# Two more modulation units summed on VectorE, the last two of twelve beside the down map

## What is computed

```python
silu_c  = jax.nn.silu(c)        # for the latent tokens
silu_cc = jax.nn.silu(c_ctx)    # for the context tokens
for i in range(DEPTH):          # DEPTH = 2
    mx = jnp.split((silu_c  @ ada_w[i] + ada_b[i])[:, None, :], 6, axis=-1)
    mc = jnp.split((silu_cc @ ada_w[i] + ada_b[i])[None, None, :], 6, axis=-1)
    hx = _modulate(_rms_norm(x,   norm_w[i, 0]), mx[0], mx[1])
    hc = _modulate(_rms_norm(ctx, norm_w[i, 0]), mc[0], mc[1])
    ...
```

## Time and profile before

| | |
|---|---|
| median of 3 runs | 2016.01 us (2014.74 to 2018.27) |
| profiled execution, its own time | 2017.62 us |
| its span | 2015.8 us |
| PE busy | 94% |
| weight loads of PE | 78% |
| DVE busy | 78% |
| ACT busy | 62% |
| chain that ended last | PE 79%, DVE 11%, issue 3%, ACT 3% |
| mean granted TensorE clock | 0.976 |

### The profile page before, as it was taken

One profiled execution on the slowest core, in us unless ns is written; L12 is line 12 of the kernel. 1 busy time (PEld: TensorE's weight loads), 2 busy tenths in 40 slices (PEclk: granted clock), 3 DMA queues, 4 the chain that ended last, 5 costly groups with the idle time before them and its releaser, 6 DMA issues.

```text
span 2015.8 us, 29074 instructions
## 1 busy us (share of the span) xinstructions
PE 1895.2 (94%) x10365; PEld 1565.4 (78%) x10366; DVE 1582.4 (78%) x1829; ACT 1259.3 (62%) x1763; POOL 188.5 (9%) x136
## 2 busy tenths in 40 slices
PE   4989889999999799998899999999999999999997
PEld 3966778888877677777787888888888888888885
DVE  2256468665665779988669999999999899999998
ACT  3336572222465445556557888888888888888885
POOL 1000000000000146456100000000000000000100
PEclk8999899999999889999989999999999999999999
DMA  9346215665455222222359999999999999999994
GB/s 340 126 168 252 84 65 198 199 208 189 152 183 171 64 63 85 64 84 84 117 196 372 372 382 380 371 386 365 393 371 377 385 364 387 367 390 374 377 395 192
DMA packets 248637, 508.50 MB, mean 252 GB/s; under 512 B 10635, under 2 KB 63195, under 8 KB 248539
## 3 DMA queue, kind: packets, MB, share of 16 engines
q1 hardware_dynamic: 246112, 499.79, 68.9%
q0 software_dynamic: 1856, 6.82, 0.9%
q10 hardware_dynamic: 571, 0.57, 0.1%
HBM read 501.38 MB, written 5.77 MB: 252 GB/s over the span
## 4 chain that ended last, share of the span: by engine, by line
PE 79%; DVE 11%; issue 3%; ACT 3%; DMA 1%; POOL 1%; ACTq 0%; SPq 0%; DVEq 0%; POOLq 0%
PE bank L836 19%; PE bank L838 18%; PE bank L837 18%; PE bank L1078 4%; PE bank L1080 4%; PE bank L1079 4%; DVE ar L2460 3%; DVE lo L2099 2%; PE bank L1159 1%; PE bank L1160 1%; PE bank L1161 1%; PE bank L1414 1%; PE bank L862 1%; ACT ar L1600 1%; DMA raw<-in_mix_in_w_dram 1%
## 5 line engine op out<-in xcount | busy, mean ns | idle before, releaser
L2099 DVE TENSOR_TENSOR lo<-raw,hi 128x1024 fp32r<-128x1024 f32 x844 | 1024.1, 1236 | 226.2 <-ACT hi L1537 151.2
L1555 ACT ACTIVATE hi<-raw 128x1024 fp32r<-128x1024 f32 x672 | 710.4, 1063 | 176.6 <-PE bank L838 174.0
L836 PE MATMUL bank<-hi,xh_t 128*128 128x512 f32 (+1 forms) x1184 | 450.0, 380 | 22.4 <-DVE lo L2099 10.8
L838 PE MATMUL bank<-hi,xl_t 128*128 128x512 f32 (+1 forms) x1184 | 446.2, 377 | 0.0
L837 PE MATMUL bank<-lo,xh_t 128*128 128x512 f32 (+1 forms) x1184 | 445.9, 377 | 0.0
L1537 ACT ACTIVATE hi<-raw 128x1024 fp32r<-128x1024 f32 x128 | 135.2, 1061 | 270.5 <-PE bank L1080 172.7
L836 PEld LDWEIGHTS bank<-hi,xh_t 128*128 128x128 f32 x1184 | 224.9, 190 | 66.7 <-issue 24.8
L838 PEld LDWEIGHTS bank<-hi,xl_t 128*128 128x128 f32 x1184 | 224.7, 190 | 40.7
L837 PEld LDWEIGHTS bank<-lo,xh_t 128*128 128x128 f32 x1184 | 225.1, 190 | 39.3
L836 PE MATMUL bank<-hi,hth 128*128 128x512 f32 x624 | 249.0, 399 | 3.1 <-DVE lo L2099 3.1
L838 PE MATMUL bank<-hi,htl 128*128 128x512 f32 x624 | 243.8, 391 | 0.0
(11 more groups left out here) (342 smaller groups left out, 2189.0 us busy)
## 6 DMA issues: line engine op xcount, KB each, us to landing
raw<-in_moe_gu_w_dram SPq DMA_DIRECT2D x224, 1024.0 KB, 7.9
raw<-in_moe_down_w_dram SPq DMA_DIRECT2D x112, 1024.0 KB, 7.7
raw<-in_ada_w_dram SPq DMA_DIRECT2D x14, 2048.0 KB, 8.6
raw<-in_ffn_gu_w_dram SPq DMA_DIRECT2D x22, 1024.0 KB, 5.2
raw<-in_ffn_down_w_dram SPq DMA_DIRECT2D x22, 1024.0 KB, 4.9
ar<-in_ada_w_dram SPq DMA_DIRECT2D x20, 1024.0 KB, 5.2
raw<-in_ssm_in_w_dram SPq DMA_DIRECT2D x16, 1024.0 KB, 5.4
raw<-in_mix_out_w_dram SPq DMA_DIRECT2D x8, 1024.0 KB, 8.6
```

Of the source, the lines that this page charges most:

```text
L836: mm(o, a_hi, w_hi, start=first, stop=False, **kw)
L838: return mm(o, a_lo, w_hi, start=False, stop=last, **kw)
L1555: A_(hi[:, p % SPL, :], raw[:, u, (p % 2) * PIECE:(p % 2 + 1) * PIECE], ACT.Copy).then_inc(m_hi, 1)
L2099: TT(lo[:, p % SPL, :], raw[:, u, h * PIECE:(h + 1) * PIECE], hi[:, p % SPL, :].bitcast(F32), ALU.subtract).then_inc(done, 1)
```

## The change

`N_RAW_ADA` goes from 14 to 12. Pairs 8 and 9 of the mixer loop lose their modulation unit, and units 12 to 23 (twelve instead of ten) are summed on DVE. Steps 1 to 4 of the up map now take units that both sides need, steps 5 to 10 one-sided ones. Units 22 and 23 come beside the down map: unit 22's halves behind `h_lo` in iterations q = 1 and 2, unit 23's in q = 6 and 7. Their loads stand ahead of those of down units 2 and 5. `ada_sums` on PE and the bias and scale work behind it on DVE move from q = 4 to q = 12, and the shapes of the sums follow the counts.

```diff
-N_RAW_ADA = 14
+N_RAW_ADA = 12
 N_SUM_ADA = N_ADA - N_RAW_ADA
+N_TWO_ADA = N_ADA // 2 + ADA_FIRST - N_RAW_ADA
...
-        red_two = m5.take(64)
+        red_two = m5.take(32 * N_TWO_ADA)
...
                 for i in range(2):
-                    load_sum(j + 1, i)
+                    if j + 1 < FFN_STEPS:
+                        load_sum(j + 1, i)
                     load_up(j + 2, i)
             for i in range(2 * FFN_STEPS):
+                if i in (2, 5):
+                    for h in range(2):
+                        load_sum(FFN_STEPS + i // 4, h)
...
-                if q == 4:
+                if q == 12:
                     ada_sums(bank[2])
...
                 if q + 4 < 2 * FFN_CHUNKS:
                     h_lo(q + 4)
-                if q == 4:
+                if q in (1, 2):
+                    ada_rows(FFN_STEPS, q - 1)
+                if q in (6, 7):
+                    ada_rows(FFN_STEPS + 1, q - 6)
+                if q == 12:
                     dve.wait_ge(ada_col, N_RAW_ADA + 1)
```

More of the change, by code:

```diff
@@ L877, in ada_sums @@
                     at = slice(32 * q, 32 * q + 32)
-                    mm(o[at, 0:16].rearrange("p (e c) -> p e c", e=4), by_32,
-                       red_two.rearrange("p (e c q) -> p e c q", e=4, q=4)[:, :, :, q],
+                    n = 8 * N_TWO_ADA
+                    mm(o[at, 0:n].rearrange("p (e c) -> p e c", c=4), by_32,
+                       red_two.rearrange("p (e c q) -> p e c q", c=4, q=4)[:, :, :, q],
                        start=True, stop=True, tile_position=(0, 32 * q))
-                    m = mm(o[at, 16:48].rearrange("p (e c) -> p e c", e=8), by_32,
+                    m = mm(o[at, n:n + 32].rearrange("p (e c) -> p e c", e=8), by_32,
                            red_one.rearrange("p (e c q) -> p e c q", e=8, q=4)[:, :, :, q],
@@ L2353, in ada_rows @@
                         r = red_two[:, 16 * (2 * e + s):16 * (2 * e + s) + 16] if len(sum_sides(a)) == 2 else \
-                            red_one[:, 16 * (e - 2):16 * (e - 2) + 16]
+                            red_one[:, 16 * (e - N_TWO_ADA):16 * (e - N_TWO_ADA) + 16]
                         own(dve.transpose(turned, asum[s]))
@@ L2382, in _ @@
                     h_lo(q + 4)
-                if q == 4:
-                    dve.wait_ge(ada_col, N_RAW_ADA + 1)
[L2385 to L2390, removed]
+                if q in (1, 2):
[3 more added lines that the diff above has]
+                if q == 12:
+                    dve.wait_ge(ada_col, N_RAW_ADA + 1)
+                    bias = cols[:, V_ADAB + 4 * N_RAW_ADA:V_ADAB + 96]
+                    two, n = 4 * N_TWO_ADA, 8 * N_TWO_ADA
+                    TT(ada[:, 1, 16 - two:16, :].rearrange("p (u c) s -> p u c s", c=4),
+                       bank[2][:, 0:n].rearrange("p (u s c) -> p u c s", s=2, c=4),
+                       bias[:, 0:two].rearrange("p (u c) -> p u c", c=4).unsqueeze(3).to_broadcast((P, N_TWO_ADA, 4, 2)), ALU.add)
+                    TT(ada[:, 1, 16:48, :], bank[2][:, n:n + 32].unsqueeze(2).to_broadcast((P, 32, 2)),
+                       bias[:, two:two + 32].unsqueeze(2).to_broadcast((P, 32, 2)), ALU.add).then_inc(ada_done, 1)
                     dve.wait_ge(ada_done, N_RAW_ADA + 1)
```

## The result

| | before | changed |
|---|---|---|
| median, 8 runs each | 2016.61 us (2014.74 to 2018.58) | 2022.8 us (2019.5 to 2025.32) |
| ratio, with its 95% interval | 1 | 1.0027 (1.0018 to 1.0036) |
| profiled execution, its own time | 2017.62 us | 2025.32 us |
| its span | 2015.8 us | 2023.4 us |
| mean granted TensorE clock | 0.976 | 0.972 |

The account below looks back on a forecast made before the run. PE, busy 94% and holding 79% of the chain, was taken as the bound. Attention's -2.2 and the down map's +6.4 gave +4.2 us on 2016.0, so 2020.2 us, range 2015.0 to 2023.5.

Parts of the forecast that it names:

- the sum: Whole kernel: attention's -2.2 us plus the down map's +6.4 us make +4.2 us.
- the loop: Down map: DVE inserts and queued weight loads delay each other in a ring, PE waits, loss 6.4 us.
- 2.72 - 1.49: Down map: PE's time a piece less DVE's work a piece; DVE was read as idle some 1.1 us of each.
- Rival 1: Down map: waits pull PE's clock to half, 1.7 us more with transposes, total 2021.9 us; chance 25%.
- Attention's 2.2: Attention, pairs 8 to 11: two modulation units leaving PE gain 2.2 us, bounds 1.6 and 4.0.
- the first part: Attention: pair 9's reduction moves from 172.18 to about 170.6, a gain of 1.6 us.
- the second: Attention: from pair 9's to pair 10's reduction, `ada_copy` no longer holds up the block copy, a gain of 0.6 us.
- all moves forward as it is: Attention from pair 10 on: only one small `ada_b` is removed, so the gain carries forward unchanged.
- The clock rival: Down map: PE drops to half clock behind its waits, 1.7 us more with transposes, total 2021.9 us; chance 25%.
- rival 4: Attention gains nothing because the chain through ACT already ends last there; total 2022.4 us; chance 6%.
- Output map, slots, up map: Shifted ring slots delay the first up loads within 1.9 us of slack, two-sided steps 3 and 4 fit; cost zero.
- lower bound of 2.8: Down map: without queueing between loads, DVE's work still delays unit 5 and PE's piece 12, a loss of 2.8 us.

Follow-up runs that it names:

- the part alone: Kernel before, attention untouched, with units 22 and 23 loaded and summed a second time at the change's places beside the down map; 2025.97 us, ratio 1.0042.
- the kernels with fewer waits: Changed kernel without the four half loads of units 22 and 23 (2021.88 us, 1.0025), or with those loads moved behind down units 2, 4 and 5 (2021.78 us, 1.0026).
- the filled change: Changed kernel with dummy matmuls on PE in attention's gaps; 2019.1 us against 2017.98 for the kernel before, ratio 1.0004.

## Why the prediction was right, and where it was not

The measured 2022.8 us lies in the range, on the side forecast, 2.6 above the number; the loss is 6.2 us by the medians for the 4.2 of the sum. That it came out so near owes something to luck: in the profiles one term of -2.2 was missing at the output map, the clock added 1.8 in the down map and most of 0.95 before it, the loop came out 0.6 below its 6.4, and the part behind the transposes, where nothing was edited, was 1.3 shorter. The first two made the loss larger than the sum, the last two smaller. Point by point:

- **The place and the mechanism of the down map's loss: right.** Down unit 5 was predicted to go out at 540.6 and land 7.7 us later, with piece 10's high part at 548.3; it went at 541.24, landed after 7.4, and the high part came at 548.68. The trace of the changed kernel runs 1.3 us later at that point, which is what had been lost on balance before the up map, so in the prediction's own time these are 539.9 and 547.4. The prediction said waits before pieces 10, 11 and 12 of 1.7, 1.6 and 3.4; they were 1.26, 1.38 and 2.67. All three are a bit smaller, as the landing was a bit earlier. The chain worked out gave 6.4, and the part alone measured 5.84. Of the 5.3 us of waits the inserts alone make 2.9, the loads alone none, so the rest takes both. In time the split isn't as clear, since the clock fell for longer in the kernels with fewer waits. One reading was off without harm: 2.72 - 1.49 leaves DVE 1.2 us a piece, not 1.1.
- **Rival 1, that the clock falls behind the waits: right in kind, and in the profiled execution it happened as well.** The changed kernel's stretch costs 7.61; beside the part alone that is 1.8 more, and the rival had 1.7. The run shows 562 to 566 at 0.57. It is no constant: none in the part alone, two falls in the filled change.
- **Attention's 2.2: the local term right, its way to the end wrong.** Pairs 8 to 11 gained 2.6 (predicted 2.2 with bounds of 1.6 and 4.0); the first part came as worked out, 1.7 for 1.6, the second was 0.9 for 0.6. The step that failed is the sentence that from pair 10 on "all moves forward as it is". Pairs 10 to 19 have no modulation matmuls left, in both kernels, and wait 0.3 to 0.9 us at a time; whether the clock falls there shifts the output map's start by up to 4 us (211.82 against 215.69 with the same attention). The clock rival was applied to the down map only. Had the term been put at 0, the sum would have been 2022.4, as rival 4 had it, by another cause than rival 4's.
- **Output map, slots, up map: 0 predicted, 0 measured as the price of the edits** (76.94 from output map to marker in the kernel with loads but no inserts; 229.23 for 229.25 from the marker to the down map in the changed kernel, and no gap in steps 3 and 4).
- **The lower bound of 2.8** for loads that don't queue was met by the waits (2.9 and 3.0 in the two kernels that removed the queueing) and missed by the time (6.26 and 6.35). A bound worked out from waits alone leaves the clock out.

For the clock the rows come first. A wait of 0.94 us at 177.72, behind one of 0.63, is followed by 0.66 in the changed kernel, and a gap of some 3.7 us before 604.84 by 0.50. The same two waits were followed by half clock in the changed kernel and in three more with its attention, and by 1.00 in two (the one with sums but no loads, and the one with its sums in the up map). The Trainium skill, "TensorE: Matmul & The Clock Gate", Part 1, "What's actually happening", says that what the clock shows depends on how busy PE has recently been, and that its phase differs between runs of the same kernel. This case agrees with the first in that filling PE's waits held the clock; with the second it is in keeping, though no run shows a phase: the same two waits had either outcome, and the kernel before was timed between 2011.56 and 2020.8 us over all its executions, its shortest times with a mean clock of 0.979 to 0.980, its longest with 0.972 to 0.974. The same page's section "HAM oscillation" takes long idle gaps as what hurts; here half clock also followed gaps under 1 us among small matmuls.

What stays open. Which of the down map's waits is followed by half clock isn't settled: the part alone had four waits and no fall, the changed kernel the same four and one fall behind the last, the filled one a fall behind its first and one behind its last, the kernels with fewer waits one longer fall. Nor is it settled whether the thinner attention of the change makes the early falls more frequent: of six profiles with it and no dummies five show at least one before 200, of two with the attention of before one does.

## What to carry to other kernels

Count the slack where the side work is to stand, not the engine's average idle time. A ring two units deep took 14.9 us of inserts in seven iterations only by making PE wait; put such work in steps whose slack holds it whole (the same two sums cost 0 beside the up map and 5.8 us beside the down map). A bulk load issued right ahead of one that is due cost nothing as long as DVE had its lead, and lengthened PE's waits from 3.0 to 5.3 us when the inserts had taken that lead. When a change thins PE's row without shortening its chain, count the gaps it leaves, and price them with the clock; a saved wait isn't saved time if half clock follows. Dummy matmuls in such gaps are cheap and worth trying where a profile shows stretches of small matmuls at half clock: here 34 of them alone took 0.2% off the kernel before, and 40 took the version with its sums in the up map from 0.05 to 0.28% below that kernel.

## What the runs showed of the hardware

- PE's granted clock fell to 1.2 GHz behind gaps of only 0.6 and 0.9 us between small matmuls in four of six executions of the same attention (0.66 over 5 us and 0.57 over 8 us in two of them), stayed at 2.4 GHz behind the same gaps in the other two, and stayed there through the whole stretch in all four kernels whose gaps were filled with 34 to 56 dummy matmuls.
- A single run tells little of this: the same program's time moved over 9 us (2011.56 to 2020.8, on more than one chip; 8.3 on one) with the mean clock between 0.980 and 0.972, more than the change is worth.
- Two 1 MB loads 1.25 us apart on one queue landed after about 5 and 7.4 to 7.6 us, one alone after 4.8 to 4.9, in up map and down map alike. With the modulation load moved from ahead of it, down unit 5 landed after 4.9.
